# Stick-breaking attention: suffix sums on TensorE replaced by a running sum along the keys on VectorE

## The reference

```python
logits = einsum("td,sd->ts", q, k) * Dh ** -0.5
mask = s_idx < t_idx                                   # strictly earlier keys
log_keep = where(mask, log_sigmoid(-logits), 0.0)
after = sum(log_keep, -1) - cumsum(log_keep, -1)       # keys behind s, up to t
wts = where(mask, exp(log_sigmoid(logits) + after), 0.0)
o = einsum("ts,sd->td", wts, v)                        # then o * silu(z), @ w_out
```

## Time and profile before

| | us |
|---|---|
| median of 3 runs | 1206.02 (1204.51 to 1206.64) |
| the profiled execution | 1202.77 |
| its span, first to last instruction | 1200.7 |

### The profile page before, as it was taken

One profiled execution on the slowest core, in us unless ns is written; L12 is line 12 of the kernel. 1 busy time (PEld: TensorE's weight loads), 2 busy tenths in 40 slices (PEclk: granted clock), 3 DMA queues, 4 the chain that ended last, 5 costly groups with the idle time before them and its releaser, 6 DMA issues.

```text
span 1200.7 us, 21271 instructions
## 1 busy us (share of the span) xinstructions
PE 1157.6 (96%) x8914; PEld 906.3 (75%) x8914; DVE 492.0 (41%) x920; ACT 536.7 (45%) x920; POOL 370.8 (31%) x148
## 2 busy tenths in 40 slices
PE   5999999999989999999999999999999999999998
PEld 4688886677768889778776666898887777678767
DVE  4575544554313373260214553463302332230563
ACT  4232246744336343552457675343225433754530
POOL 0133441322255333434341000413244132343161
PEclk9999999999999999999999999999999999999999
DMA  9723222276731232123423110223232421324201
GB/s 318 245 71 105 85 90 71 86 254 217 219 112 37 70 106 70 70 70 105 116 88 97 27 27 1 70 89 105 84 109 72 114 77 39 106 70 150 99 1 70
DMA packets 105376, 120.42 MB, mean 100 GB/s; under 512 B 5144, under 2 KB 91704, under 8 KB 105288
## 3 DMA queue, kind: packets, MB, share of 16 engines
q1 hardware_dynamic: 101424, 116.14, 30.5%
q10 hardware_dynamic: 3864, 3.01, 0.9%
HBM read 110.75 MB, written 2.10 MB: 94 GB/s over the span
## 4 chain that ended last, share of the span: by engine, by line
PE 84%; ACT 6%; DVE 4%; issue 3%; DMA 1%; ACTq 0%; SPq 0%; POOL 0%; DVEq 0%
PE ps L2067 41%; PE ps L2874 4%; PE ps L2687 3%; PE ps L2678 2%; PE ps L2113 2%; PE ps L2455 2%; PE ps L2208 2%; PE ps L2691 2%; PE ps L2717 2%; PE ps L2151 1%; PE ps L2231 1%; PE ps L2284 1%; PE ps L2840 1%; PE ps L2482 1%; PE ps L2827 1%
## 5 line engine op out<-in xcount | busy, mean ns | idle before, releaser
L613 POOL TENSOR_TENSOR wlo<-raw,whi 128x2048 fp32r<-128x2048 f32 x53 | 245.1, 4625 | 562.6 <-ACT whi L777 550.2
L777 ACT ACTIVATE whi<-raw 128x2048 fp32r<-128x2048 f32 x52 | 99.3, 1911 | 191.1 <-PE ps L2067 152.6
L619 POOL TENSOR_TENSOR wlo<-raw,whi 128x2048 fp32r<-128x2048 f32 x10 | 46.4, 4644 | 111.0 <-ACT whi L866 62.7
L1285 ACT ACTIVATE p<-sc,nmx 128x256 f32<-128x256 f32 x64 | 32.0, 501 | 45.8 <-PE ps L2827 44.7
L1894 DVE CUSTOM_DVE_ANT_0 sc<-ps,biast 128x256 f32<-128x256 f32 (+1 forms) x64 | 22.4, 393 | 65.7 <-PE ps L2816 36.7
L866 ACT ACTIVATE whi<-raw 128x2048 fp32r<-128x2048 f32 x11 | 21.1, 1917 | 62.7 <-PE ps L2067 62.7
L2067 PE MATMUL ps<-hC_hi,whi 128*128 128x512 f32 x184 | 47.0, 397 | 0.8 <-POOL wlo L613 0.8
L2067 PE MATMUL ps<-hC_lo,whi 128*128 128x512 f32 x184 | 45.5, 390 | 0.0
L2067 PE MATMUL ps<-hC_hi,wlo 128*128 128x512 f32 x184 | 45.4, 389 | 0.0
L2067 PEld LDWEIGHTS ps<-hC_hi,whi 128*128 128x128 f32 x184 | 33.7, 188 | 14.8 <-issue 6.4
L2067 PEld LDWEIGHTS ps<-hC_lo,whi 128*128 128x128 f32 x184 | 34.5, 188 | 7.4
(11 more groups left out here) (531 smaller groups left out, 2839.2 us busy)
## 6 DMA issues: line engine op xcount, KB each, us to landing
raw<-in_w_in_dram SPq DMA_DIRECT2D x24, 1024.0 KB, 5.2
raw<-in_w_in_a_dram SPq DMA_DIRECT2D x16, 1024.0 KB, 5.7
raw<-in_w_ada_dram SPq DMA_DIRECT2D x8, 1024.0 KB, 5.1
late_w<-in_w_ada_dram SPq DMA_DIRECT2D x8, 1024.0 KB, 6.4
raw<-in_w_kv_dram SPq DMA_DIRECT2D x8, 1024.0 KB, 5.1
raw<-in_w_in_b_dram SPq DMA_DIRECT2D x8, 1024.0 KB, 5.3
ada_a<-in_w_ada_dram SPq DMA_DIRECT2D x4, 1024.0 KB, 10.1
ada_b<-in_w_ada_dram SPq DMA_DIRECT2D x4, 1024.0 KB, 13.1
```

Of the source, the lines that this page charges most:

```text
L613: pool.tensor_tensor(wlo[:, s, :], raw[:, s, :], whi[:, s, :].bitcast(F32), ALU.subtract).then_inc(lo_ready, 1)
L619: pool.tensor_tensor(wlo[:, s, :], raw[:, s, :], whi[:, s, :].bitcast(F32), ALU.subtract).then_inc(lo_ready, 1)
L777: A(whi[:, s, :], raw[:, s, :], ACT.Copy).then_inc(hi_ready, 1)
L1285: A(p2[:, n % 2, 256 * e:256 * e + 256], sc2[:, n % 2, 256 * e:256 * e + 256], ACT.Exp, scale=-1.0, bias=nmx[:, grp, t, 2 * hp + e:2 * hp ...
```

## The change

The arithmetic is turned round. With keep = sigmoid(-l) and take = sigmoid(l), the running sum from the last key down, A_s = keep_s * A_(s+1) + take_s, is one minus the product of all keeps from s on; the weight of key s is A_s - A_(s+1). Summed by parts, o = sum over s of A_s * (v_s - v_(s-1)). So:

- Queries now lie on the partitions and keys along the free axis. The work goes in 24 rounds, three to a pair of heads: query tile 3 (512 keys), tile 2 (384), tiles 1 and 0 (256 and 128), each for both heads at once.
- PE makes the scores of a round for both heads in the two row halves (no swapped copies of K and Q, so the 32 DMAs of `swap` go), and adds the mask.
- ACT makes two sigmoids of every score, and copies the transposed sums out of PSUM. Its exp, log and abs passes go. A table of sigmoid takes the place of that of exp and log.
- DVE runs one `tensor_tensor_scan` for each head and query tile, backwards over the keys: 64 in all, over 511, 383, 255 or 127 keys. Its maximum, absolute-value and block-sum instructions go.
- PE transposes the sums, 128 by 128 (20 for a pair, into banks 4 and 5), and multiplies them with differences of V, 128 columns at a time. The suffix sums on PE go.
- V's differences are made once: SP copies V one row down (`v_down`, 2 MB, ahead of the load of block 16), POOL clears row 0 (after the low parts of block 13) and subtracts (four instructions of 128x1024, after those of block 16).
- The list on PE: `scores(0)` comes ahead of all of `last_gate`; then in iteration r `scores(r)`, `turns(r-2)`, `valued(r-3)`. The products of the output projection for k = 0 and 1 stand ahead of the last `valued`.

The core of the diff (what is removed is the text of the functions named above):

```diff
@@ sync
+                if r == load_of["dense", D_ZB]:
+                    sp.wait_ge(v_done, 8)
+                    sp.wait_ge(dense_full, 4 * (D_VB + 2))
+                    sp.dma_start(v_down[1:128, :, :], Vb[0:127, :, :]).then_inc(v_shifted, 16)
+                    sp.dma_start(v_down[0:1, 1:NT, :], Vb[127:128, 0:NT - 1, :]).then_inc(v_shifted, 16)
                 load(r)
@@ gpsimd
             for d in range(D_OUTA + 1, D_OUTB):
                 for s in range(1 if d in own_parts else 2):
                     split_lo(d, s)
+                if d == D_VB + 1:
+                    pool.wait_ge(dense_full, 4 * (D_VB + 2))
+                    pool.memset(v_down[0:1, 0, :], 0.0).then_inc(v_diff, 1)
+                if d == D_ZB:
+                    pool.wait_ge(v_diff, 1)
+                    pool.wait_ge(v_shifted, 32)
+                    for j in range(NT):
+                        pool.tensor_tensor(Vb[:, j, :], Vb[:, j, :], v_down[:, j, :], ALU.subtract).then_inc(v_diff, 1)
@@ scalar
+            def keeps(r):
+                act.wait_ge(scores_full, r + 1)
+                if r >= 3:
+                    act.wait_ge(scan_done, r - 2)
+                if r == 0:
+                    act.wait_ge(v_diff, 1 + NT)
+                A(of_round(kept, r), logits(r), ACT.Sigmoid, scale=-1.0).then_inc(kept_done, 1)
+            def takes(r):
+                if r >= 3:
+                    act.wait_ge(turned_full, r - 2)
+                A(of_round(taken, r), logits(r), ACT.Sigmoid).then_inc(taken_done, 1)
+            def turned_out(r):
+                act.wait_ge(turned_full, r + 1)
+                if r >= 2:
+                    act.wait_ge(pv_full, r - 1)
+                A(turned(r)[:, 0:ends * width(r)]..., ps[:, 4:4 + ends, 0:width(r)], ACT.Copy).then_inc(turned_act, 1)
+            for r in range(ROUNDS + TURNED):        # 24 + 2
+                if r < ROUNDS:
+                    keeps(r)
+                    takes(r)
+                if r >= TURNED:
+                    turned_out(r - TURNED)
+                if r == 1:
+                    next_hi(D_ZB + 1, 1)
+                if r == 3:
+                    act.wait_ge(gate_done, 8)
+                    A(ybt[:, 1, :], zsT[:, KD - 1, :], ACT.Sigmoid).then_inc(last_silu, 1)
+                if r >= YB + 1 and (r - YB - 1) % 3 == 0:
+                    yb_hi((r - YB - 1) // 3)
@@ vector
+            def scans(r):
+                dve.wait_ge(kept_done, r + 1)
+                dve.wait_ge(taken_done, r + 1)
+                for s in range(2):
+                    for i, at in round_tiles(r):
+                        a = width(r) * s + at
+                        keys = slice(a + 128 * i + 126, a - 1 if a else None, -1)
+                        last = dve.tensor_tensor_scan(taken[:, r % 3, keys], kept[:, r % 3, keys], taken[:, r % 3, keys],
+                                                      0.0, ALU.mult, ALU.add)
+                last.then_inc(scan_done, 1)
@@ tensor
+            def turns(r):
+                pe.wait_ge(scan_done, r + 1)
+                if r:
+                    pe.wait_ge(turned_act, r)
+                for e in range(2):
+                    for b in range(width(r) // 128):
+                        at = width(r) * e + 128 * b
+                        last = pe.transpose(ps[:, 4 + e, 128 * b:128 * b + 128], taken[:, r % 3, at:at + 128], ident)
+                last.then_inc(turned_full, 1)
+            scores(0)
+            last_gate(range(12))
+            scores(1)
+            last_gate(range(12, 24))
+            for r in range(2, ROUNDS + VALUED):     # 24 + 3
+                if r < ROUNDS:
+                    scores(r)
+                if TURNED <= r < ROUNDS + TURNED:
+                    turns(r - TURNED)
+                if r == ROUNDS + VALUED - 1:
+                    first_out_b(range(2))
+                if r >= VALUED:
+                    valued(r - VALUED)
+            first_out_b(range(2, KD - 1))
+            first_out_b(range(KD - 1, KD))
```

More of the change, by code:

```diff
@@ L1180, in _ @@
                 A(zsT[:, 4 + j, :], dense[j], ACT.Silu).then_inc(gate_done, 1)
[L1183 to L1205, removed]
+            nc.scalar.preload_act_table_set(SIGMOID)
+            def keeps(r):
[13 more added lines that the diff above has]
+                    act.wait_ge(pv_full, r - 1)
+                ends = 1 if shared_out(r) else 2
+                A(turned(r)[:, 0:ends * width(r)].rearrange("p (e n) -> p e n", e=ends), ps[:, 4:4 + ends, 0:width(r)],
+                  ACT.Copy).then_inc(turned_act, 1)
             def yb_hi(kt):
@@ new lines, in turned_second @@
+            def turned_second(r):
+                dve.wait_ge(turned_full, r + 1)
+                if r >= 2:
+                    dve.wait_ge(pv_full, r - 1)
+                copy(turned(r)[:, width(r):2 * width(r)], ps[:, 5, 0:width(r)]).then_inc(turned_dve, 1)
+            for r in range(ROUNDS + TURNED):
+                if r < ROUNDS:
+                    scans(r)
+                if r >= TURNED and shared_out(r - TURNED):
+                    turned_second(r - TURNED)
+                if r == 0:
@@ L2656, in last_gate, with scores @@
                         last.then_inc(dense_full, 1)
-            last_gate(range(8))
             pe.wait_ge(kqn_done, 16)
             pe.wait_ge(bf_ready, 1)
[L2663 to L2667, removed]
+            def scores(r):
+                kt = r // 3
+                if r == 0:
                     pe.wait_ge(gate_done, 7)
[L2669 to L2681, removed]
-                last.then_inc(qk_full, 1)
@@ L2707, in weighted @@
-            def weighted(kt, blocks):
-                pe.wait_ge(wt_done, 4 * kt + 4)
-                if kt >= 2:
+                if r >= 2:
+                    pe.wait_ge(taken_done, r - 1)
+                for i, at in round_tiles(r):
+                    for e in range(2):
+                        mm(logits(r)[:, e, at:at + 128 * i + 128], qTb[side(e), kt, 128 * i:128 * i + 128],
+                           kTb[side(e), kt, 0:128 * i + 128], start=at == 0, stop=True, skip_group_check=True)
@@ L2711, in weighted, with valued @@
+            def valued(r):
+                kt = r // 3
+                pe.wait_ge(turned_act, r + 1)
+                if shared_before(r + 1):
+                    pe.wait_ge(turned_dve, shared_before(r + 1))
+                if r % 3 == 0 and kt >= 2:
                     pe.wait_ge(yb_done, kt - 1)
-                if kt == 1:
+                if r == 3:
                     pe.wait_ge(gate_done, 8)
-                for j in blocks:
-                    for n in (2 * kt, 2 * kt + 1):
-                        rs = slice(64 * (n % 2), 64 * (n % 2) + 64)
-                        last = mm(ps[rs, 6 + kt % 2, 128 * j:512], Vb[:, j, 64 * n:64 * n + 64],
-                                  att(n, off[j], off[j] + 512 - 128 * j), start=j == 0, stop=True,
-                                  skip_group_check=True)
@@ L2720, in weighted @@
-                if blocks[-1] == 2:
-                    last.then_inc(pv_full, 1)
+                for i, at in round_tiles(r):
+                    for j in range(i + 1):
+                        for e in range(2):
+                            n = 2 * kt + e
+                            last = mm(ps[side(e), 6 + kt % 2, 128 * i:128 * i + 128], Vb[:, j, 64 * n:64 * n + 64],
+                                      turned(r)[:, width(r) * e + at + 128 * j:width(r) * e + at + 128 * j + 128],
+                                      start=j == 0, stop=j == i, skip_group_check=True)
```

172 lines of the change are left out of this document (51 added, 121 removed).

## The result

The changed kernel takes 1239.47 us (median of 4 runs, 1237.35 to 1240.47), the kernel before, on the same chip, 1205.26 (4 runs, 1204.48 to 1206.64). The ratio is 1.028, with a 95% interval of 1.0262 to 1.0298: slower by 34 us where 1193 was forecast. The profiled execution took 1238.93 us, its span is 1236.9.

A forecast was written before the change was run, and what follows sets the result against it. PE was taken to bound the attention. A gain of 20.9 us there, less stalls of 4.5, 1.7 and 2.0, gave -12.7: 1190.1 from the profiled 1202.77, or 1193 as median, 3.25 higher; range 1182 to 1205.

The forecast's parts named there:

- the last of the costs ahead of the attention: SP's 2 MB copy of V, ahead of block 16's loads: needs some 10 us, through in time, no cost.
- PE's list: PE's attention work per pair of heads: scores 2.7, masks 0.46, transposes 4.4, `valued` 3.0, in sum 10.6 us.
- The start: Start of the attention: PE stops 1.1 us before `scores(0)`, plus 2 us of ramp in the first rounds.
- ACT and DVE: Attention, per pair: ACT 8.9 us, DVE 5.3 to 18.7 with the lower end taken, both below PE's 10.6.
- The memset: POOL's list before block 14: the wait for block 13 and the memset cost PE 4.5 us, the halved clock 1.7.
- POOL against DVE: Before block 17: POOL's subtractions and low part may hold up two DVE instructions; 2 us taken, 0 to 4 possible.
- Half given back: Attention: ACT or DVE becomes the bound, 11.8 us a pair, 9.6 us given back, 1203 us; chance 0.13.
- the scan as the bound: Attention: DVE's scans bound above 3.1 ns a key, 1215 us at 4.2 ns, 1258 at 6.3; chance 0.08.
- The clock in the transposes: Attention: PE counts as idle in transposes and falls to 1.2 GHz, 84.7 us more, 1278 us; chance 0.03.
- No stalls: Ahead of the attention: POOL's order hurts nobody, 20 us gained, 1186 us; chance 0.10.
- Slower: Whole kernel: a time above 1208.4 us, more than 0.2% over the kernel before; chance 0.11.

The follow-up runs named there:

- a1: The changed kernel with its 127-partition copy of V split into copies of 112 and 15 partitions: 1180.44 us, 0.9789 of the kernel before.
- b1: The kernel before plus the 127-partition copy of V alone, on SP's queue, read by nothing but awaited by the first head: 1267.95 us, 1.0503 of before.
- a5: a1 with the memset and V's four subtractions moved to DVE and 8 of 24 `last_gate` products ahead of `scores(0)`: 1169.5 us, 0.9726 of before.
- a3: a1 with V's four subtractions done by DVE instead of POOL: 1175.6 us, 0.9762 of the kernel before.
- a6: a1 with every transpose made twice, the result being the same: 1195.88 us, 0.9945 of the kernel before.
- c1: The kernel before plus the 127-partition copy of V, unread, issued from ACT's queue instead of SP's: 1268.96 us, 1.053 of before.

## Why the prediction was wrong

**The step that failed is the last of the costs ahead of the attention**: "the 2 MB copy goes out behind block 15's loads and about 13 us ahead of block 16's. At the time that a 1 MB load takes to land ... it needs some 10, so it is through in time". At its measured 27 GB/s it needs 77, since the copy of 127 partitions ran on one DMA engine and the load of 128 partitions, by which I priced it, on sixteen. The cost is 56.5 us of waiting and 2.2 of clock (a1, and b1 from the other side). I priced a transfer by its bytes, and gave this step no rival. The Trainium skill (DMA: Bandwidth & Descriptors, Why a DMA increments its semaphore by 16 and not by 1) has the rule that was needed: the number of engines is the largest one up to 16 that divides the slowest dimension of both sides, and it names 127 partitions as a case of one. The runs agree: 127 partitions went on one engine at 27 GB/s, 124 on four, 112 with 15 at 299 GB/s.

Without that step the forecast would have been off the other way. a1's span is 22.3 us under that of before, where the sum said 12.7, and its 1180.4 us lie below the range of 1182 to 1205. Term by term:

- **PE's list**, 10.6 us a pair forecast, 8.62 measured. Scores 2.7 against 2.75, masks 0.46 against 0.77 (each group has an entry of its own), `valued` 3.0 against 2.64. The mis-sized term is the transposes, 4.4 against 2.38. The earlier trace rows calls its eight records four transposes, and I took two records for each. They are eight transposes: two calls of four stand side by side there. The kernel before makes 32 transposes in that line, and its trace has 32 records (ns each, least, median and most), so the right price could have been read before:

```profile
L2514 PE MATMUL ps<-cs,osb x32: 270/273/329, 372.6 to 400.7; 128*128 128x128 f32 x32
```

  Eight pairs at 2.0 are 16 us, more than the 14.5 by which the attention did better (35.4 against 20.9); the masks took back 2.5 and `valued` gave 2.9.
- **The start.** PE waited 0.8 us ahead of `scores(0)`, forecast 1.1. In the first rounds PE waited 1.2, 1.1 and 0.9 us for sums and their copies (the rows are those shown under a5, and the changed kernel has the same three), 3.2 against the 2.0 I gave them.
- **ACT and DVE.** Busy time of PE, PEld, DVE, ACT and POOL in the pair shown above, and the groups of the scans and of one of ACT's passes (line, engine, shapes, count, busy us, mean ns, idle before):

```profile
727.35:735.97 8.62, 8.55 (x86) 5.92 (x86) 7.20 (x10) 7.69 (x12) 0.00 (x0) 1.00 0.01 2
```

```profile
L1802 DVE TENSOR_TENSOR_SCAN taken<-kept,taken 128x511 f32<-128x511 f32 x16 | 18.7, 1207 | 30.0 <-ACT taken L1202 30.0
...
L1202 ACT ACTIVATE taken<-ps 128x768 f32<-128x768 f32 x16 | 13.0, 814 | 0.0
...
L1802 DVE TENSOR_TENSOR_SCAN taken<-kept,taken 128x127 f32<-128x127 f32 x16 | 6.3, 395 | 0.0
```

  ACT is busy 7.69 us a pair, forecast 8.9. A pass is as long as forecast (814 ns over 768 columns), but the 8.9 was a sum of lengths, and passes that follow each other overlap: two of 768 columns start at 726.63 and 727.32, 0.69 apart. At 8.9 ACT would have been over the 8.62 that PE came to need, so that PE stays the bound rests on ACT's term having been too high as well. DVE's scans take 2.12 ns a key, and DVE is busy 7.20 us a pair with `yb` and `yb_low`, within the 3.1 ns a key that I had as the bound. My own value, 1.04, was half of it; it changed nothing, as PE stayed the bound.
- **The memset**: 4.5 us of wait and 1.7 of clock forecast, 4.3 and 1.7 measured. The method, following POOL's list past the new wait to the instruction that PE needs, gave the size.
- **POOL against DVE**: 2 us taken, 0 to 4 bounded; it cost 3.4 and another 2.7 of clock behind it, 6.1. The two DVE instructions took 6.71 us against 3.25 in the kernel before. The first (1.71 us) got through where POOL's last subtraction ended, at 669.55, and the second (5.08) only where the low part behind it ended, at 674.5. That the two engines shut each other out of a port is argued; a3 shows that the wait of PE goes when POOL no longer subtracts. I had the place and the wait of the worse case, and no clock term for it, though I had one for the memset.

**The rivals.** None was what happened. "Half given back" and the scan as the bound are refuted by a chain of PE's lines alone. The clock in the transposes is refuted too: 1.00 from 720 to 760, with transposes for 2.38 of every 8.62 us, and in a6, with twice as many, 1.00 from 670 to 710. What I cited for it from the Trainium skill (TensorE: Matmul & The Clock Gate, Part 4: PE-mode transpose) is not refuted by that, since the products between them may keep the clock up; a stretch of transposes alone was not run. "No stalls" was wrong about both stalls. Slower came true with 0.11 given to it, but by none of the mechanisms that it was given for: the slower side had its weight on the new arithmetic, and the loss came from a copy.

## What to carry to other kernels

Price a DMA by the number of engines it is cut over before its bytes: here a transfer on 127 partitions ran on one of sixteen, and what it delays is every load that has a share on that engine, from whatever queue; cut it at a partition count with a large divisor of at most 16. When a list gains a wait or an instruction, follow it to the next thing that the bound engine needs, and add the halved clock behind each stall of PE. An operation that the trace doesn't show in its exact form wants a price from both sides even where its term is only part of a sum that seems safe.

## What the runs showed of the hardware

- One DMA engine alone copies inside SBUF at 27 GB/s in packets of 16 KB. With four at work each moved about 17 GB/s (69 to 73 together).
- Two queues on one engine take turns packet for packet (31 to 31 in 20 us), though one had packets of 1 KB and the other of 16 KB, so the first gets one seventeenth of the bytes.
- Issuing can block too, where the slow DMA stands in the same queue: SP was held 36.9 us in issuing a 12 KB DMA behind the copy, and 26 and 41 us in issuing two loads in b1. With the copy in ACT's queue (c1) each of SP's issues took 0.37 us.
- A scan costs 2.12 ns a key, (1207 - 395) / (511 - 127), and some 0.13 us for each instruction. The Trainium skill (DVE: opcode table, instruction layouts, handler registers and perf-mode slots, Datapath and trigger behaviour) says half throughput; against 1.04 ns a column of two-input instructions the trace agrees.
- An fp32 transpose of 128 columns is one record and costs PE 0.11 us (eight in 0.88; by a6 0.10), half of a product of that width, which is two records of 0.107.
- Two DVE instructions with two SBUF inputs each, 3.25 us in the kernel before, took 6.71 beside POOL's last subtraction and the low part behind it: the first got in between the two, the second waited out the low part.
- Passes of ACT that follow each other overlap: 814 ns long, 0.69 us from start to start.
